# Joining the 32-row blocks of a chunked delta rule inside the recurrence

## The reference

```python
qkv, a, bb, z = split_cols(h @ w_in, IN_C_SIZES)        # then causal conv, width 4, and SiLU
q = l2norm(split_heads(q, ...)) * (G_DK ** -0.5)        # sums of squares over the 128 channels
k = l2norm(split_heads(k, ...))
...
def gdn_chunk(S0, inp):
    G = jnp.cumsum(g, axis=-1)
    decay = jnp.exp(jnp.where(incl, G[..., :, None] - G[..., None, :], -jnp.inf))
    A = beta[..., :, None] * jnp.einsum('bhlk,bhsk->bhls', k, k) * decay * strict
    sol = triangular_solve(A + eye(L), rhs, lower=True, unit_diagonal=True)
    u = sol[..., :dv] - einsum(sol[..., dv:], S0)
    o = exp(G) * (q @ S0) + ((q @ k.T) * decay) @ u
    S1 = exp(G_end) * S0 + (k * exp(G_end - G)).T @ u
```

## Time and profile before

| | us |
|---|---|
| median of 3 runs | 4383.95 |
| lowest, highest | 4382.75, 4391.84 |
| profiled execution, its own time | 4390.73 |
| its span, first to last instruction | 4389.0 |
| mean granted clock of TensorE over the span | 0.908 of full |
| TensorE busy | 3978.0 (91%) |
| VectorE busy | 1718.6 (39%) |
| ScalarE busy | 1079.1 (25%) |
| GpSimd busy | 384.7 (9%) |

### The profile page before, as it was taken

One profiled execution on the slowest core, in us unless ns is written; L12 is line 12 of the kernel. 1 busy time (PEld: TensorE's weight loads), 2 busy tenths in 40 slices (PEclk: granted clock), 3 DMA queues, 4 the chain that ended last, 5 costly groups with the idle time before them and its releaser, 6 DMA issues. The chain is left out here.

```text
span 4389.0 us, 47463 instructions
## 1 busy us (share of the span) xinstructions
PE 3978.0 (91%) x17693; PEld 2313.4 (53%) x17693; DVE 1718.6 (39%) x3095; ACT 1079.1 (25%) x2791; POOL 384.7 (9%) x561
## 2 busy tenths in 40 slices
PE   6999999996889999889999489999999986757998
PEld 2555555553255555555554345544445456655665
DVE  0222222222145555444443134343434357534564
ACT  1111111110134444311111213323131233311222
POOL 0000000000000000000000010000000011004542
PEclk9999999998779999978788599999999987658999
DMA  7211111115431000022221501111111136437653
GB/s 280 68 51 51 50 50 50 48 41 183 118 93 26 22 18 18 27 100 63 71 64 44 189 25 51 51 46 60 41 63 36 53 101 157 111 95 247 189 185 97
DMA packets 325171, 365.84 MB, mean 83 GB/s; under 512 B 119783, under 2 KB 245170, under 8 KB 322810
## 3 DMA queue, kind: packets, MB, share of 16 engines
q1 hardware_dynamic: 286486, 311.13, 23.2%
q0 software_dynamic: 7536, 26.09, 2.1%
q10 hardware_dynamic: 30964, 26.13, 2.0%
HBM read 233.61 MB, written 129.67 MB: 83 GB/s over the span
## 5 line engine op out<-in xcount | busy, mean ns | idle before, releaser
L394 PE MATMUL a_bank<-a_w_in,a_hT 128*128 128x512 f32 (+5 forms) x2176 | 779.9, 514 | 5.6 <-ACT a_qT L533 3.4
L1718 PE MATMUL d_bank<-d_hT,d_w_in 128*128 128x512 f32 (+1 forms) x1920 | 743.0, 542 | 5.9 <-ACT d_hT L1777 5.9
L394 PEld LDWEIGHTS a_bank<-a_w_in,a_hT 128*128 128x128 f32 (+1 forms) x2176 | 383.7, 188 | 374.9 <-issue 319.9
L1718 PEld LDWEIGHTS d_bank<-d_hT,d_w_in 128*128 128x128 f32 x1920 | 342.9, 198 | 353.0 <-issue 352.9
L888 PE MATMUL c_ps<-c_kT,c_q 96*128 96x512 f32 (+5 forms) x688 | 306.2, 580 | 22.1 <-DMA c_kT<-scratch_kT 10.6
L1724 PE MATMUL d_bank<-d_w_in,d_hT 128*128 128x512 f32 (+3 forms) x816 | 277.8, 491 | 0.0
L1244 PE MATMUL m_bank<-m_w_out,m_mixT 128*128 128x512 f32 (+1 forms) x544 | 272.0, 659 | 1.3 <-ACT m_mixT L1352 1.3
L1846 DVE SCALAR_TENSOR_TENSOR d_cv<-d_xb,k_wconv,d_cv 128x512 f32<-128x512 f32 (+1 forms) x360 | 237.0, 658 | 12.8
L2598 PE MATMUL r_bank<-r_w_out,r_mixT 128*128 128x512 f32 (+1 forms) x544 | 236.3, 592 | 2.1 <-ACT r_mixT L2637 2.1
L1844 DVE TENSOR_SCALAR d_cv<-d_xb,k_wconv 128x512 f32<-128x512 f32 (+1 forms) x120 | 52.8, 440 | 434.5 <-ACT d_xb L1788 426.3
L1019 DVE TENSOR_REDUCE c_part<-c_ps 128x1 f32<-128x1024 f32 (+9 forms) x144 | 137.7, 960 | 186.3 <-PE c_ps L888 183.9
(11 more groups left out here) (345 smaller groups left out, 4713.0 us busy)
## 6 DMA issues: line engine op xcount, KB each, us to landing
r_kv<-scratch_qkv SPq DMA_DIRECT2D x17, 1024.0 KB, 5.7
scratch_qkv<-d_ts SPq DMA_DIRECT2D x64, 256.0 KB, 2.3
p_wada<-in_a_w_ada SPq DMA_DIRECT2D x3, 4096.0 KB, 25.9
b_wada<-in_c_w_ada ACTq DMA_DIRECT2D x3, 4096.0 KB, 24.1
d_w_in<-in_c_w_in SPq DMA_DIRECT2D x6, 2048.0 KB, 12.9
l_kT<-scratch_g_kT SPq DMA_DIRECT2D x17, 512.0 KB, 5.7
l_qT<-scratch_g_qT SPq DMA_DIRECT2D x17, 512.0 KB, 6.3
r_kT<-scratch_g_kT SPq DMA_DIRECT2D x17, 512.0 KB, 5.2
```

The costliest lines, as they stand in the source:

```text
L394: mm = nc.tensor.matmul(o[:n, 0:w], hT[u][:, k, :n], w_in[:, k, c0:c0 + w], start=(k == 0), stop=(k == KD - 1))
L1718: mm = nc.tensor.matmul(o[:, 0:w.w], w_in[:, k, w.a * P:(w.a + 1) * P], hT[w.r % 2][:, k, 0:w.w], start=(k == 0), stop=(k == KD - 1))
```

## The change

In `project_c` the squares of queries, their products with ones and the copies of the sums go. `local` gets them back in another form: ScalarE squares the turned queries of a tile (`sq`), TensorE multiplies them with ones (`qq`, 8 matmuls of 8 columns), VectorE writes `K["eq"]`.

`local` keeps E, KK, qk and the masks, in plain order of tiles, with two buffers for nA, and stores nA (`g_nA`). It solves the first three batches (12 tiles of the prompt). The joins leave `local`. `recur` loads nA and the solved 32-row blocks, joins those of tile t + 1 between the pieces of the projection of tile t - 1, and solves the last two batches (tiles 12 to 15, and the sample) in VectorE's stream during tiles 1 to 4 and 6 to 9. The solver's code is moved into a class and computes as before. ke and vb are made in place in kv, so the load of kv waits for their last readers.

```diff
-CONST_NAMES = ["ident", "upto", "after", "before", "neg", "diag", "ones",
-               "lev1", "lev2", "lev4", "lev8", "lev16", "lev32", "lev64"]
+CONST_NAMES = ["ident", "upto", "after", "neg", "diag", "ones"]
+BATCHES = [[4 * k + j for j in range(4)] for k in range(NT // 4)] + [[TS]]
+SOLVED = 3
...
 # project_c, TensorE
-                    if w.a < GH:
-                        pe.wait_ge(squared, w.q + 1)
-                        if w.q >= 1:
-                            pe.wait_ge(sums_out, w.q)
...
-                        for j in range(w.tiles):
-                            mm = nc.tensor.matmul(psc[:n, c0 + 8 * j:c0 + 8 * j + 8], sq[w.q % 2][:, j * n:(j + 1) * n], ones[:, 0:8],
-                                                  start=True, stop=True)
-                        mm.then_inc(summed, 1)
 # project_c, VectorE
-                        nc.vector.tensor_tensor(sq[q % 2][:, 0:w.w], sl[u][:, 0:w.w], sl[u][:, 0:w.w], ALU.mult).then_inc(squared, 1)
...
-                    nc.vector.tensor_copy(K["ss"][:n, t0:t0 + m, w.a],
-                                          psc[:n, c0:c0 + 8 * m].rearrange("p (j e) -> p j e", e=8)[:, :, 0]).then_inc(sums_out, 1)
...
+class Solver:
+    def load(self, sp, g_D, k, j):
+        if j == 0 and k >= self.bufs:
+            sp.wait_ge(self.T_ready, k - self.bufs + 1)
+        sp.dma_start(self.B[k % self.bufs][j * 32:(j + 1) * 32, 0:1024], g_D[self.batches[k][j]]).then_inc(self.in_[k % self.bufs], 16)
+    def store(self, sp, g_T, g_TTd, k):
+        n, m0 = 32 * len(self.batches[k]), 32 * self.batches[k][0]
+        sp.wait_ge(self.T_ready, k + 1)
+        sp.dma_start(g_T[m0:m0 + n, :], self.T[k % self.bufs][:n, 0:1024]).then_inc(self.st_T, 16)
+        sp.wait_ge(self.TT_ready, k + 1)
+        sp.dma_start(g_TTd[m0:m0 + n, :], self.TT[:n, :]).then_inc(self.st_TT, 16)
+    def step(self, dve, k, part):      # parts 0 to 3: blocks8, blocks16 and the halves of blocks32 of before
...
 # local, order of the PSUM banks and of TensorE
-        for i in range(TILES - LAG):
-            a = i + LAG
-            work += [("X32", i), ("E", a), ("TT32", i), ("KK0", a), ("X64", i), ("KK1", a), ("TT64", i), ("qk", a)]
+        order = [("sums", 0)] + [(n, a) for a in range(TILES) for n in ("E0", "E1", "KK0", "KK1", "qk0", "qk1", "qq")]
...
+            def lengths(t):
+                o, fill = claim(pe, "qq", t)
+                pe.wait_ge(squared, t + 1)
+                for h in range(GH):
+                    mm = nc.tensor.matmul(o[:, h * 8:(h + 1) * 8], sq[t % 2][:, h, :], const["ones"][:, 0:8], start=True, stop=True)
+                mm.then_inc(fill, 1)
...
+            for t in range(TILES):             # ScalarE
+                decays(t)
...
+                nc.scalar.activation(sq[t % 2][:, :, :], qT[t % LOADS][:, :, :], ACT.Square).then_inc(squared, 1)
+                if t >= 8 and t % 4 == 0 and t // 4 - 2 < SOLVED:
+                    solver.turn(act, t // 4 - 2)
...
+            for t in range(TILES):             # VectorE
+                key_scores(t)
+                query_scores(t)
+                if t >= 4 and t // 4 - 1 < SOLVED:
+                    solver.step(dve, t // 4 - 1, t % 4)
...
 # recur, loads
+            def load_blocks(t):
...
+                sp.dma_start(nA[u][0:64, :, :], sc["g_nA"][t][0:64]).then_inc(lv_in[u], 16)
+                sp.dma_start(nA[u][64:96, :, 96:128], sc["g_nA"][t][64:96, :, 96:128]).then_inc(lv_in[u], 16)
+                for r in range(4):
...
+                    sp.dma_start(TT[u][quarter(r), :, quarter(r)], src).then_inc(lv_in[u], 16)
+                for r, c in ((0, 0), (1, 1), (2, 0)):
...
+                    sp.dma_start(Tc[u][quarter(r), :, quarter(c)], src).then_inc(lv_in[u], 16)
...
+            sp.wait_ge(cleared, 6)
+            load_blocks(0)
+            load_turned(0)
             load_kv(0)
-            load_turned(0)
+            for j in range(4):
+                solver.load(sp, sc["g_D"], 0, j)
             load_z(0)
+            load_blocks(1)
+            load_turned(1)
+            load_kv(1)
             sp.dma_start(w_out[:, :, :], io["c_w_out"].rearrange("(k p) n -> p k n", p=P)).then_inc(w_in, 16)
-            load_kv(1)
-            load_turned(1)
...
                 if t + 2 < TILES:
-                    sp.wait_ge(ke_ready, t + 1)
-                    sp.wait_ge(vb_ready, t + 1)
+                    sp.wait_ge(r_ready, 2 * (t + 1))
+                    done(sp, "dS1", t)
                     load_kv(t + 2)
...
                     load_turned(t + 2)
+                    load_blocks(t + 2)
                     sp.wait_ge(mix_ready, t + 1)
                     load_z(t + 2)
+                if t == 5:
+                    solver.store(sp, sc["g_T"], sc["g_TTd"], 0)
+                    solver.load(sp, sc["g_D"], 1, 0)
...
 # recur, TensorE, after AU of tile t (the joins are the small matmuls of before)
+                if more:
+                    couple32(t + 1)
                 if t >= 1:
-                    project(t - 1, 0)
-                    project(t - 1, 1)
+                    project(t - 1, 0, 0)
+                    project(t - 1, 0, 1)
+                if more:
+                    join32(t + 1)
+                if t >= 1:
+                    project(t - 1, 1, 0)
+                if more:
+                    couple64(t + 1)
+                if t >= 1:
+                    project(t - 1, 1, 1)
+                if more:
+                    join64(t + 1)
...
 # recur, VectorE, after mix of tile t
+                if t + 1 < TILES:
+                    join32(t + 1)
+                if 1 <= t <= 4 or 6 <= t <= 9:
+                    solver.step(dve, t // 6, (t - 1) % 5)
                 if t >= 1:
                     add_y(t - 1, 1)
...
 # recur, GpSimd
-            for m in TT + aT:
+            for m in TT + Tc:
+                nc.gpsimd.memset(m[:, :, :], 0.0).then_inc(cleared, 1)
+            pool.wait_ge(cleared, 4)
+            for m in aT:
                 nc.gpsimd.memset(m[64:128, :, 0:64], 0.0).then_inc(cleared, 1)
```

More of the change, by code:

```diff
@@ L2095, in products, with decays @@
                 mm.then_inc(fill, 1)
[L2097 to L2105 removed]
+            def decays(t):
@@ new lines, in _ @@
+            n = TILES * GH
+            for j, name in enumerate(("upto", "after", "ones")):
+                mm = nc.tensor.matmul(o[:, j * n:(j + 1) * n], const[name], gg[:, :, :].rearrange("p t h -> p (t h)"),
+                                      start=True, stop=True)
+            mm.then_inc(fill, 1)
+            for t in range(TILES):
+                v = t % LOADS
+                decays(t)
+                pe.wait_ge(kT_in[v], 16 * (t // LOADS + 1))
+                products("KK0", t, kT[v], kT[v])
+                products("KK1", t, kT[v], kT[v])
+                pe.wait_ge(qT_in[v], 16 * (t // LOADS + 1))
+                products("qk0", t, kT[v], qT[v])
+                products("qk1", t, kT[v], qT[v])
+                lengths(t)
@@ L2279, in _ @@
-            for a in range(TILES):
-                masks(a)
         @block.vector
@@ new lines, in _, with key_scores @@
+            solver.begin(dve)
+            def key_scores(t):
+                u = t % 2
+                for c in GR:
+                    o, free = take(dve, f"KK{c}", t)
+                    dve.wait_ge(masked, 2 * t + c + 1)
+                    if c == 0 and t >= 2:
+                        dve.wait_ge(st_D[u], 64 * (t // 2))
+                        dve.wait_ge(st_nA[u], 32 * (t // 2))
+                    nc.vector.scalar_tensor_tensor(nA[u][:, heads(c), :], view(o), -1.0, M[u][:, heads(c), :],
@@ L2434, in recur @@
         mixT = sb("mixT", [P, KD, P])
+        nA = [sb(f"nA{u}", [P, GH, P]) for u in range(2)]
+        Tc = [sb(f"Tc{u}", [P, GH, 64]) for u in range(2)]
+        Xe = sb("Xe", [P, GH, 32])
+        X64 = sb("X64", [P, GH, 64])
+        solver = Solver(nc, ctx, "r_", BATCHES[SOLVED:], 1)
         yg = sb("yg", [P, D])
@@ L2454, in recur @@
         BANK = {"KS0": 0, "U0": 0, "KS1": 1, "U1": 1, "QS0": 2, "AU0": 2, "QS1": 3, "AU1": 3, "dS0": 4, "dS1": 5,
-                "mixT0": 6, "y0": 6, "mixT1": 7, "y1": 7}
-        order = []
+                "mixT0": 6, "y0": 6, "mixT1": 7, "y1": 7, "X32": 0, "T32": 5, "T10": 4, "X64": 1, "T64": 4}
+        LEVELS = ("X32", "T32", "T10", "X64", "T64")
+        PAIRS = ((0, 1), (2, 3))
+        order = [(n, 0) for n in LEVELS]
         for t in range(TILES + 1):
@@ L2739, in final, with join32 @@
                                                ALU.mult, ALU.mult).then_inc(y_ready, 1)
+            def join32(t):
+                o, free = take(dve, "T32", t)
+                for r, q in PAIRS:
+                    ins = nc.vector.tensor_copy(TT[t % 2][quarter(r), :, quarter(q)], narrow(o)[quarter(r)])
+                ins.then_inc(free, 1)
+            solver.begin(dve)
+            join32(0)
             for t in range(TILES):
```

665 lines of the change are left out of this document (263 added, 402 removed).

## The result

| | before | after |
|---|---|---|
| median of the runs | 4386.64 us (4382.75 to 4391.84) | 4261.21 us (4258.68 to 4272.92) |
| ratio | | 0.9719, 95% interval 0.9697 to 0.974 |
| profiled execution: span | 4389.0 us | 4271.2 us |

What follows compares the result with a forecast made beforehand. TensorE bounds the body of `recur`; `local` waits on chains. Projection -57, `local` -174, joins +81, solving +12, clock +4, start +14 sum to -120 us: 4265 us forecast, 8 in 10 for 4225 to 4330.

Steps and rivals of the forecast that it cites:

- the passes, the clock and the narrow turns: Projection, TensorE: 27 us for passes of 32 wide turns, some 11 of clock put back, 2 for narrow turns.
- the ring: `local`: ScalarE and TensorE chain of Relu, Exp, Square, `qq`, next E; 8.5 to 11 us a tile, taken as 10.
- the last stores: `local`, its end: 8 us in the stage's sum of 189 us.
- Rival 2: `local` held by TensorE at the lower clock: 262 us instead of 189, total 4338; chance 0.12.
- Rival 1: `recur` loses its clock: 29 us more a tile if at half throughout, 4700; chance 0.08, 0.05 of it ending slower.
- Parts 0: `recur`, first part of a batch's solving on VectorE: costs nothing.
- part 1: `recur`, second part of a batch's solving on VectorE: costs 0.7 us.
- parts 2 and 3: `recur`, long solver parts on VectorE delay R, for which U waits: 2.2 us and 0.5 for R's second half.
- I add 4 (0 to 10): `recur`: 4 us for a lower clock behind the pauses from solver parts, range 0 to 10.
- the two terms together: `recur`, solving two batches: 12 us of waits and 4 us for the clock behind them.
- the clears, the bytes and the many small loads: Start of `recur`: 4 us of clears, 2.4 for 0.76 MB more, 2 to 3 for small loads; +9.
- the chain by T64: Start of `recur`: T64 of tile 1 waits for VectorE's T32 copy behind mix of tile 0, delaying KS: +5 us.

Runs made afterwards that it cites:

- the run with E ahead: Changed kernel with TensorE computing E of the next tile ahead of qq of this one in `local`: 4253.17 us, ratio 0.9704.
- the run in one block: Changed kernel with the next tile's five joins in one block between AU and the projection, their copies moved too: 4370.97 us, ratio 0.9963.
- The pieces: Changed kernel with solver parts 1 to 3 in `recur` cut in two, one piece behind the sums of o: 4250.21 us, ratio 0.9698.

## Why the prediction was right

**The projection: right.** -58.6 against -57. The waits for `k_ss` are gone; those for the normalised x rose from 25.8 to 33.8 us, so 18 of the 26.4 us stayed won, where the prediction kept 17 for this very reason. TensorE's busy time there fell from 1074.5 to 1034.1 us (view by stretches), by the 40 us that the passes, the clock and the narrow turns were put at. The run with the sums put back gives the 57 us back, and shows that the sums cost `local` 14, so moving them is worth some 43.

**`local`: right by its steps, and 4 us too short.** The ring was taken at 10 us: E of tiles 2 to 5 stands 9.9 to 10.0 us apart, and the run with E ahead shows that it was the ring. The first part came at 56.5 us (58.5 in the sum), VectorE's twelve parts took 124.1 us (117 and 6 of waits), and from the last part to the next stage it was 12.3 us where 8 had been set for the last stores. Rival 2 (TensorE at the lower clock, 262 us) did not come: the clock was 0.80. What the sum of the stage hides: 54 us of the gain come by the two batches, and by difference about 115 by the joins, levels and stores that left.

**The joins: right.** 5.38 us a tile against 5.43. With the groups that they slow they come to 1.3, 1.6, 1.3 and 1.2 us, where 1.22, 1.63, 1.29 and 1.29 were said. Rival 1, the lost clock, did not come, for the reason given against it; the run in one block shows the same products losing it as soon as they wait for each other. The Trainium skill (TensorE: Matmul & The Clock Gate, "HAM oscillation — how this bites in real kernels") says that waits between bursts put the array back to half rate; the rows of that run agree in kind, with shorter waits than those of the page's example, and the steady tile of the changed kernel has no such wait.

**The solver in `recur`: right in its place, its two halves mis-sized.** Parts 0 cost nothing, part 1 some 0.9 us, parts 2 and 3 a wait of 2.25 and 2.15 us in front of U, as said. The waits sum to 9.1 us where 12 were forecast, and the slower passes behind them cost the other 9.4 of the 18.5 where "I add 4 (0 to 10)" stood. In the six traces with this body of `recur` the waits are 8.8 to 9.6 us and the rest 5.6 to 9.8, so the 16 of the two terms together was met, and their split was not. The pieces show that both go when the waits go.

**The start of `recur`: right in size, by two terms that were not.** +18.6 less one tile's joins is +13 against +14. But U of tile 0 came 27.2 us after the first clear instead of 12.2: +15.0, where the clears, the bytes and the many small loads were put at +9. kv of tile 0, now behind the clears and the blocks, reached GpSimd 20.5 us after the first clear instead of 5.1 (order of time, GpSimd, before and after):

```profile
3941.75 1.90 POOL L2685 TENSOR_TENSOR r_ke<-r_kv,r_wk 128x1024 f32<-128x1024 f32 x1 [1.71 <-DMA r_kv<-scratch_qkv]
```

```profile
3725.24 1.90 POOL L2624 TENSOR_TENSOR r_kv<-r_kv,r_wk 128x1024 f32<-128x1024 f32 x1 [15.26 <-DMA r_kv<-scratch_qkv]
```

From there to U of tile 1 it took only 1.3 us longer, where the chain by T64 was put at +5. That chain (T64 behind the T32 copy, behind mix) is the longest wait, 18.9 us, and z(1) its root; but the kernel before waited nearly as long at the same place, for R behind the same mix (order of time, TensorE, U of tile 1 before):

```profile
3986.53 2.05 PE L2580 MATMUL r_bank<-r_R,r_TT 128*128 128x128 f32 x8 [16.26 <-DVE r_R L2750]
```

That the two errors cancel is luck. The run with z(1) early shows that the transfers behind it allowed no more than 2.4 us of the long wait.

**The sum.** -118 against -120 for the two profiled executions, and no stage is off by more than 5.3 us (`local`), so the total is no luck between large errors. That it fits to 2 us is closer than the runs repeat: the medians differ by 125 us. The range for 8 in 10, up to 4330, was said to reach rival 2, which stood at 4338; it does not.

## What to carry to other kernels

Here small dependent products cost a busy TensorE little more than their passes when each waits out its copies behind a piece of a long product; in a block of their own the same products cost nearly the whole gain. Work moved under another engine's bound is free only up to the slack at its own place in the queue: count from the landmark to the consumer, and cut what is longer into pieces for the other gaps. When a stage starts with clears, issue first the loads that need none.

## What the runs showed of the hardware

A product of VectorE over two operands from SBUF took 1.96 us in the changed kernel, and 2.76 where the pieces put it beside GpSimd's z product (order of time, VectorE and then GpSimd, in the run in pieces):

```profile
3834.15 2.76 DVE L1922 TENSOR_TENSOR r_prod<-r_B,r_T 128x1024 f32<-128x1024 f32 x1
```

```profile
3832.74 2.35 POOL L2631 TENSOR_TENSOR r_z<-r_z,k_g_gout 128x1024 f32<-128x1024 f32 x1
```

The two overlap from 3834.15 to 3835.09, 0.94 us, and the product is 0.80 longer. In the next tile a product of the same size overlaps by 1.10 us and takes 2.87 us instead of 1.89. The Trainium skill (SBUF — State Buffer, "Who interferes with whom") says that such instructions exclude each other, and these rows agree.

The same wait on TensorE did not always cost it its clock. Behind the wait of 2.25 us above, 16 passes ran at the lower of the two clock levels (3.65 us instead of 1.95); behind one of 2.14 us, at the same place in the run with E ahead, 16 passes took 2.44 us, and the granted clock was 1.00 from 3860 to 3900 us:

```profile
3876.20 2.44 PE L2423 MATMUL r_bank<-r_R,r_TT 128*128 128x128 f32 x16 [2.14 <-DVE r_R L2701]
```

The six traces with this body of `recur` have 24 such waits of 2.08 to 2.32 us. 15 of these tiles took 32.9 to 33.5 us from KS to KS and nine took 31.7 to 31.9; what decides between the two stays open. Behind waits of 0.94, 0.56 and 0.73 us between small products the clock fell too (0.50, the run in one block), while 80 passes of 32x32 and 32 of 64x64 in a tile, without waits, left every large group at the upper level (a 16-pass group 1.95 us).
